# Stick-breaking attention of a hybrid decoder step: one head at a time, or both heads of a query block side by side

## The reference, cut to what matters

```
def _sb_block(q, k, v, bias, q_pos, k_pos):
    """Stick-breaking weights for one query block. q: [B,H,Q,d]; k, v: [B,H,K,d] (f32); bias: [H]."""
    z = jnp.einsum('bhqd,bhkd->bhqk', q, k) * (SB_HEAD_DIM ** -0.5) + bias[None, :, None, None]
    mask = k_pos[None, :] < q_pos[:, None]
    log_beta = jax.nn.log_sigmoid(z)
    log_rest = jnp.where(mask, jax.nn.log_sigmoid(-z), 0.0)
    tail = lax.cumsum(log_rest, axis=3, reverse=True) - log_rest
    A = jnp.where(mask, jnp.exp(log_beta + tail), 0.0)
    return jnp.einsum('bhqk,bhkd->bhqd', A, v)
...
    proj = h @ W['w_in'][l]
    qa, fa, ia, ga, qb, kb, vb, uc, gl = jnp.split(proj, _split_points(), axis=-1)
...
    ob = _sb_attention(qb, k_all, v_all, W['sb_bias'][l], q_pos, k_pos)
...
    u = ua * jax.nn.sigmoid(ug)
    c = _causal_dwconv(u_full, W['conv_w'][l], W['conv_b'][l])
```

## Time and profile before

| | |
|---|---|
| median of 3 runs | 2314.67 us (2312.46 to 2316.16) |
| span of the profiled execution | 2321.0 us |
| TensorE matmul / weight load busy | 93% / 86% |
| VectorE / ScalarE / GpSimd busy | 46% / 26% / 25% |
| chain that ended last | TensorE 85%, VectorE 7%, ScalarE 5% |
| the four groups, A and B stage together | 1098.6 us, 99.4 to 1198.0 |

### The profile page before, as it was taken

One profiled execution on the slowest core, in us unless ns is written; L12 is line 12 of the kernel. 1 busy time (PEld: TensorE's weight loads), 2 busy tenths in 40 slices (PEclk: granted clock), 3 DMA queues, 4 the chain that ended last, 5 costly groups with the idle time before them and its releaser, 6 DMA issues.

```text
span 2321.0 us, 31837 instructions
## 1 busy us (share of the span) xinstructions
PE 2147.9 (93%) x12704; PEld 2005.6 (86%) x12704; DVE 1079.1 (46%) x1169; ACT 604.1 (26%) x760; POOL 589.4 (25%) x392
## 2 busy tenths in 40 slices
PE   6999999999999999999978889789999999999994
PEld 5887898878988899878968889579999999999993
DVE  4277555775367663765534652452222223222235
ACT  3234412343223432345123421220100101001011
POOL 1221112211111211211112232343232333323322
PEclk9997999989998999989989999899999999999997
DMA  4220204102131121312144333201111120111132
GB/s 141 57 93 28 58 28 127 52 19 67 47 114 37 48 56 58 101 39 58 38 159 149 111 102 120 102 14 55 32 50 41 41 59 29 52 45 36 54 106 79
DMA packets 203987, 156.89 MB, mean 68 GB/s; under 512 B 15730, under 2 KB 188402, under 8 KB 203890
## 3 DMA queue, kind: packets, MB, share of 16 engines
q1 hardware_dynamic: 201698, 146.89, 20.4%
q10 hardware_dynamic: 2192, 8.65, 1.0%
HBM read 120.16 MB, written 35.35 MB: 67 GB/s over the span
## 4 chain that ended last, share of the span: by engine, by line
PE 85%; DVE 7%; ACT 5%; issue 1%; DMA 1%; POOL 0%; POOLq 0%; SPq 0%; DVEq 0%; ACTq 0%
PE psum L364 69%; PE psum L601 4%; PE psum L621 3%; PE psum L666 3%; PE psum L612 2%; PE psum L569 1%; DVE hid L1482 1%; PE psum L648 1%; DVE mix L1467 1%; PE psum L630 1%; DVE arena L1170 1%; DVE x_again L1461 0%; DMA conv_full<-c_d 0%; DVE hid_lo L1484 0%; DVE mix L1457 0%
## 5 line engine op out<-in xcount | busy, mean ns | idle before, releaser
L364 PE MATMUL psum<-h_hi,w_hi 128*128 128x352 f32 x2400 | 541.7, 334 | 37.1 <-DVE h_lo L1174 10.9
L364 PE MATMUL psum<-h_hi,w_lo 128*128 128x352 f32 x2400 | 525.7, 327 | 0.0
L364 PE MATMUL psum<-h_lo,w_hi 128*128 128x352 f32 x2400 | 525.6, 328 | 0.0
L364 PEld LDWEIGHTS psum<-h_hi,w_hi 128*128 128x128 f32 x2400 | 412.1, 193 | 75.9 <-issue 53.1
L364 PEld LDWEIGHTS psum<-h_hi,w_lo 128*128 128x128 f32 x2400 | 419.8, 191 | 0.0
L364 PEld LDWEIGHTS psum<-h_lo,w_hi 128*128 128x128 f32 x2400 | 416.3, 192 | 0.0
L341 POOL CAST w_hi<-w_raw 128x1024 fp32r<-128x1024 f32 x60 | 71.9, 1198 | 913.7 <-PE psum L364 895.1
L354 POOL CAST w_hi<-w_raw 128x512 fp32r<-128x512 f32 (+1 forms) x128 | 96.5, 754 | 732.5 <-PE psum L364 643.3
L356 POOL TENSOR_TENSOR w_lo<-w_raw,w_hi 128x512 fp32r<-128x512 f32 (+1 forms) x128 | 229.7, 1794 | 10.3
L1140 ACT ACTIVATE hid<-psum 128x1056 f32<-128x1056 f32 x32 | 33.7, 1054 | 583.1 <-PE psum L364 583.1
L364 PE MATMUL psum<-hid_hi,w_hi 128*128 128x352 f32 x768 | 166.4, 325 | 10.8 <-DVE hid_lo L1484 10.8
(11 more groups left out here) (226 smaller groups left out, 2459.8 us busy)
## 6 DMA issues: line engine op xcount, KB each, us to landing
w_raw<-in_w_in SPq DMA_DIRECT2D x60, 512.0 KB, 4.0
w_raw<-in_w_ff SPq DMA_DIRECT2D x32, 512.0 KB, 4.0
w_raw<-in_w_ff SPq DMA_DIRECT2D x64, 256.0 KB, 2.7
g_d<-gate_logits SPq DMA_DIRECT2D x24, 528.0 KB, 2.7
gates<-g_d SPq DMA_DIRECT2D x24, 528.0 KB, 3.6
arena<-in_xT SPq DMA_DIRECT2D x8, 528.0 KB, 7.0
x_again<-in_xT SPq DMA_DIRECT2D x1, 4224.0 KB, 13.8
x_d<-x_again ACTq DMA_DIRECT2D x8, 528.0 KB, 2.7
```

The source lines that it names most:

```text
L364: mm = pe.matmul(ps[:, b0 + g, 0:GW], w[:, slot, k, :], x[:, k, g * GW:(g + 1) * GW], start=(k == 0 and w is wh and x is xh), stop=(k == k ...
```

## The change

Scores and values of a query block q are done for both heads at once. `scores(p, q, c)` computes a chunk of up to 512 keys for head 0 into bank 3 and for head 1 into bank 4, in pieces of 256 that alternate between the two (partitions 0 to 63 and 64 to 127 of q and k). Blocks 4 to 7 have two chunks; since both heads take one bank each, chunk 1 can only be computed once ScalarE has read chunk 0. `values(p, q)` alternates the heads' 64-column tiles for each key block. The buffers for that are a fourth `zb` (the tile `ug`) and a second staged transpose (the tile `ua`), both free once the convolution input is formed.

The A stage now loops over q = 0 to 8. The units are given out by contraction tile: `fill(n)` does the next n tiles. In each q TensorE does: scores of chunk 0, transposes of block q-1 head 0, 2 tiles, scores of chunk 1 (q >= 4), sample work, 2 tiles, transposes of block q-1 head 1, 3 tiles, values of block q-1, 1 tile. That is one unit per q, nine in the A stage instead of eight. In the B stage 40 tiles are left for the 12 places (4, 4, then eight times 3, then 4, 4).

On ScalarE, each q begins with the copy of unit q-1 and ends with the exp of block q, head 1. VectorE in each q masks, taps and clips head 0, then head 1, taps, tail sum of head 0, taps, tail sum of head 1: four taps as in two steps before.

The diff, cut to its core:

```
+QB = TP // P
+Z_CHUNKS = [q if q < 4 else 4 + 2 * (q - 4) for q in range(QB + 1)]
+A_FILL = (2, 2, 3, 1)
+H_FILL = (4, 4, 3, 3, 3, 3, 3, 3, 3, 3, 4, 4)
...
-            def scores(p, i):
...
+            def scores(p, q, c):
+                chunk = Z_CHUNKS[q] + c
+                if chunk:
+                    z_read.wait(pe, p, 2 * chunk)
+                n = min(512, P * (q + 1) - 512 * c)
+                for a in range(0, n, 256):
+                    w = min(256, n - a)
+                    for e in range(2):
+                        rows = slice(DH * e, DH * e + DH)
+                        mm = pe.matmul(ps[:, 3 + e, a:a + w], qT[rows, q * P:(q + 1) * P],
+                                       kT[rows, 512 * c + a:512 * c + a + w], start=True, stop=True)
                 mm.then_inc(z_ready.sem, 1)
...
+            def values(p, q):
+                at_ready.wait(pe, p, 2 * q + 2)
+                if q:
+                    o_read.wait(pe, p, q)
+                for kb in range(q + 1):
+                    for e in range(2):
+                        mm = pe.matmul(ps[DH * e:DH * e + DH, 7, (q % 4) * P:(q % 4 + 1) * P],
+                                       vtok[:, kb, DH * e:DH * e + DH], atv[e][:, kb * P:(kb + 1) * P],
+                                       start=(kb == 0), stop=(kb == q))
                 mm.then_inc(av_done.sem, 1)
...
+                at_k = [0]
+                def fill(n):
+                    for _ in range(n):
+                        jj, k = divmod(at_k[0], KD)
+                        if jj < units(more):
+                            unit_part(PRE + jj, p, (k,))
+                            at_k[0] += 1
...
+                for q in range(QB + 1):
+                    if q < QB:
+                        scores(p, q, 0)
+                    if q == 1:
                         v_staged.wait(pe, p, 1)
+                    if q:
+                        turn_a(p, 2 * q - 2)
+                    fill(A_FILL[0])
+                    if 4 <= q < QB:
+                        scores(p, q, 1)
+                    if q == 1:
                         sample_scores(p)
+                    if q == 3:
                         sample_turn(p)
+                    if q == 4:
                         sample_values(p)
+                    fill(A_FILL[1])
+                    if q:
+                        turn_a(p, 2 * q - 1)
+                    fill(A_FILL[2])
+                    if q:
+                        values(p, q - 1)
+                    fill(A_FILL[3])
...
+                for q in range(QB + 1):
+                    if q:
+                        stage_unit(q - 1, p, more)
+                    if q < QB:
+                        if q == 1:
+                            u_ready.wait(act, p, 1)
+                        read_scores(q, 0)
+                    if q:
+                        stage_at(q - 1, 0)
+                    if 4 <= q < QB:
+                        read_scores(q, 1)
+                    if q < QB:
+                        softplus(q, 0)
...
+                    if q:
+                        stage_at(q - 1, 1)
+                    if q < QB:
+                        softplus(q, 1)
+                        weights_of(q, 0)
...
+                    if q:
+                        av_done.wait(act, p, q)
...
+                    if q < QB:
+                        weights_of(q, 1)
+                if more:
+                    kv_stored.wait(act, p, 32)
+                stage_unit(8, p, more)
...
-                    if j in (0, 2, 4):
-                        stage_unit(A_UNITS + j // 2, p, more)
+                    if j in (0, 3):
+                        stage_unit(9 + j // 3, p, more)
...
+                def scores_read(q, e):
+                    i, n = 2 * q + e, P * (q + 1)
+                    z, l = zb[2 * (q % 2) + e][:, 0:n], lb[e][:, 0:n]
+                    z_read.wait(dve, p, 2 * Z_CHUNKS[q + 1] - 1 + e)
...
+                for q in range(QB):
+                    scores_read(q, 0)
+                    scores_read(q, 1)
...
                     tap()
+                    tail_sum(q, 0)
+                    tap()
+                    tail_sum(q, 1)
```

More of the change, by code:

```diff
@@ L589, in _ @@
             ats = A(A_ATS, 192).rearrange("p (g n) -> p g n", g=3)
-            def scores(p, i):
-                qb, e = divmod(i, 2)
-                rows = slice(DH * e, DH * e + DH)
-                if i:
-                    z_read.wait(pe, p, i)
-                if i == 8:
-                    zs_read.wait(pe, p, 1)
-                nk = P * (qb + 1)
-                for a in range(0, nk, 512):
-                    n = min(512, nk - a)
-                    mm = pe.matmul(ps[:, 3 + a // 512, 0:n], qT[rows, qb * P:(qb + 1) * P], kT[rows, a:a + n],
-                                   start=True, stop=True)
+            def scores(p, q, c):
[9 more added lines that the diff above has]
+                                       kT[rows, 512 * c + a:512 * c + a + w], start=True, stop=True)
                 mm.then_inc(z_ready.sem, 1)
@@ L611, in turn_a @@
                 for kb in range(i // 2 + 1):
-                    mm = pe.transpose(banks(5, 1024)[:, kb * P:(kb + 1) * P], zb[i % 3][:, kb * P:(kb + 1) * P], ident)
+                    mm = pe.transpose(banks(5, 1024)[:, kb * P:(kb + 1) * P],
+                                      zb[2 * (i // 2 % 2) + i % 2][:, kb * P:(kb + 1) * P], ident)
                 mm.then_inc(t_done.sem, 1)
-            def values(p, i):
-                qb, e = divmod(i, 2)
-                at_ready.wait(pe, p, i + 1)
-                if e == 0 and qb:
-                    o_read.wait(pe, p, qb)
-                for kb in range(qb + 1):
-                    mm = pe.matmul(ps[DH * e:DH * e + DH, 7, (qb % 4) * P:(qb % 4 + 1) * P],
-                                   vtok[:, kb, DH * e:DH * e + DH], atv[:, kb * P:(kb + 1) * P],
-                                   start=(kb == 0), stop=(kb == qb))
+            def values(p, q):
[7 more added lines that the diff above has]
+                                       start=(kb == 0), stop=(kb == q))
                 mm.then_inc(av_done.sem, 1)
@@ L911, in stage_unit @@
                     stage(PRE + jj, p, *B_DST[jj - A_UNITS])
-            zb = [A(o, 1024) for o in A_Z]
+            zb = [A(o, 1024) for o in A_Z] + [ug[:, 0:1024]]
             lb = [A(o, 1024) for o in A_L]
@@ new lines, in read_scores, with softplus @@
+                def read_scores(q, c):
+                    z_ready.wait(act, p, Z_CHUNKS[q] + c + 1)
+                    n = min(512, P * (q + 1) - 512 * c)
+                    for e in range(2):
+                        act.activation(zb[2 * (q % 2) + e][:, 512 * c:512 * c + n], bank(3 + e, n), IDN,
+                                       bias=sbp[:, e:e + 1]).then_inc(z_read.sem, 1)
+                def softplus(q, e):
+                    i, l = 2 * q + e, lb[e][:, 0:P * (q + 1)]
+                    e_ready.wait(act, p, i + 1)
+                    act.activation(l, l, ACT.Exp).then_inc(exp1.sem, 1)
+                    exp1.wait(act, p, i + 1)
+                    act.activation(l, l, ACT.Ln, bias=1.0).then_inc(ln_ready.sem, 1)
@@ L1007, in group @@
                 qk_ready.wait(act, p, 1)
-                if more:
-                    kv_stored.wait(act, p, 32)
-                    u_ready.wait(act, p, 1)
                 for j in range(NL):
@@ L1025, in group @@
                     .then_inc(kdt_staged.sem, 1)
-                stage_unit(A_UNITS + 4, p, more)
+                stage_unit(12, p, more)
                 if more:
@@ L1039, in group @@
                 act.activation(A(B_RS, T), A(B_RS, T), ACT.Exp, scale=-0.5).then_inc(rs_ready.sem, 1)
-                stage_unit(A_UNITS + 5, p, more)
+                stage_unit(13, p, more)
                 if more:
@@ L1269, in group @@
                 t_done.wait(dve, p, 16)
-                av_done.wait(dve, p, 16)
+                av_done.wait(dve, p, QB)
                 os_done.wait(dve, p, 1)
```

164 lines of the change are left out of this document (58 added, 106 removed).

## The result

The changed kernel takes **2381.4 us** (median of 4 runs, 2380.9 to 2382.7) against 2315.4 us of the kernel before beside it: a ratio of **1.0284, 95% interval 1.0269 to 1.0299**, 66 us slower. The profiled execution spans 2380.9 us against 2321.0.

A forecast was written before the change was run, and what follows sets the result against it. A chain through VectorE's block and ScalarE's exp and copy was to bind late A-stage turns. A 183.2 plus B 100.4 made 283.6 us a group, 9 over 274.65; four groups add 36 to 2314.7, giving 2351 us, range 2303 to 2386.

The forecast's parts named there:

- The mechanism: A stage, q = 5 to 8: TensorE waits at the unit's first tile for ScalarE's copy, 15 to 20 us a group.
- F(5): Moment TensorE starts unit 5's first tile, after its wait for ScalarE's copy of unit 4; forecast 22.0 us after unit 4's.
- the ring: A-stage chain per turn: unit tiles, scores, read, VectorE's block, exp, copy, next unit; 23.1 to 23.2 us for q = 7.
- case D: The forecast itself: TensorE waits for the unit copy in q = 5 to 8; 2325 to 2378 us, chance 0.60.
- rival C: Score and value half tiles run one after the other, not together: 8 us a group more, 2384 us, chance 0.12.
- The walk up to F(4): Group 1's A stage summed turn by turn until TensorE starts unit 4's first tile: 71.8 us.
- cache wait: A stage, second turn: the sample's scores wait for the last cache page load, 3.4 us.
- the split: GpSimd's splitting of the next weights slows VectorE's tail sums beside it; taken as 0.8 us a turn.
- The clock: TensorE's clock halves after a stop of 6 us; 1.7 us each for q = 6, q = 7 and the tail.
- What stands behind F(8): A stage after unit 8's first tile starts: tiles, transposes and values 14.8 us, plus clock 1.7.
- Rival A: TensorE binds, not the chain: A stage 160 us, group 260.7, whole 2259 us; chance 0.06.
- Rival B: Chain binds, but clock stays up and splits cost nothing: no change, 2306 to 2325 us; chance 0.18.

The follow-up runs named there:

- kernel 1: Changed kernel with ScalarE's exp of the second head moved into the next turn, behind the unit copy and the score reads: 2288.3 us, ratio 0.9881.
- kernel 11: Fastest kernel (2218.8 us, late exp plus TensorE reordering) with the second head's exp back ahead of the unit copy: 2353.5 us, ratio 1.0157.
- kernel 3: Changed kernel with GpSimd splitting only the first of a unit's eight contraction tiles inside the groups (outputs not valid): 2333.0 us, ratio 1.0074.
- kernel 6: Changed kernel with TensorE kept busy in its three long waits by repeated score products: 2366.6 us, ratio 1.0208.
- kernel 4: Changed kernel with heads not alternated, all of head 0's score or value tiles and then head 1's: 2394.7 us, ratio 1.0337.
- kernel 5: kernel 1 with the heads' score and value tiles not alternated: 2290.9 us, ratio 0.9873.
- kernel 10: Late-exp kernel with TensorE's fills and sample steps reordered (2238.6 us), now with the heads' score and value tiles not alternated: 2248.5 us, ratio 0.9701.

## Why the prediction was right, and where it was off

**The mechanism** was forecast and is shown. The waits stand where it put them (the unit's first tile, for ScalarE's copy), three of 7 to 8 us a group, 22.8 us in sum, where "4 to 7 us, three or four times a group, 15 to 20 us in sum" was written, with VectorE busy through them. There is none at F(5), which the prediction counted in. Opening the ring by one moved instruction (kernel 1) takes them all away; closing it again under a better order elsewhere (kernel 11) brings them all back.

**The range** held by more than the mechanism. The measured 2381 us lies above the 2325 to 2378 that the prediction gave to its own case D, and nearest to the 2384 of rival C, whose mechanism the rows below refute. The stated range reached to 2386 only because C was in it: that the time fell inside is luck to that extent.

**The size.** 36 us were forecast and 66 measured. Of the 66, some 5 come from the base: the profiled execution of the kernel before was 5.6 us over its median, and the changed kernel's was not. The stages grew by 61. Term by term, for group 1, through which the prediction walked:

- The half tiles overlap fully: the timeline of the changed kernel's TensorE has a pair of value tiles every 0.11 us, each pair starting together.

```profile
549.32 0.27 PE L626 MATMUL psum<-arena 128*64 128x128 f32 x1
549.33 0.27 PE L626 MATMUL psum<-ua,arena 128*64 128x128 f32 x1
549.43 0.27 PE L626 MATMUL psum<-arena 128*64 128x128 f32 x1
549.44 0.27 PE L626 MATMUL psum<-ua,arena 128*64 128x128 f32 x1
```

  In the kernel before, one such tile alone took 0.11 us. A group's values keep TensorE busy for 9.6 us where they took 20.0, its scores for 11.0 where they took 21.8. Rival C falls.
- The walk up to F(4) was right to a microsecond: F(1) 16.2 (forecast 16.1), F(2) 36.8 (37.5, where the terms written add to 37.2), F(3) 52.9 (52.9), F(4) 72.4 (71.8), with the cache wait 2.9 us (3.4) and the sample's 3.0 (3.3). The other groups reach F(4) at 73.6 to 74.0. There the split met VectorE's second tail sum, on the ring ahead of F(1): in group 2 its scan of 128 keys took 2.52 us, in group 1 0.42. So the near hit at F(1) is group 1's luck.
- The turns from F(4) to F(8) hold **the term that was mis-sized**: 22.7, 23.8, 27.5 and 27.6 us against 22.0, 22.0, 25.3 and 25.6, 6.7 us in group 1 and 6.0 in the mean of four. Most of it is the split beside VectorE. I took 0.8 us a turn from one instruction that had met only the end of a split: it ran from 214.29 to 215.90, and the cast ahead of that subtraction ended at 215.09. The rows from F(6) to F(7) above show 0.79 on the tap that met the cast (1.03 where such a tap takes 0.24 alone) and 2.02 on the scan that started within the subtraction, 2.81 together; kernel 3 gives 2.1 to 2.7 for each turn from F(5) on, and nothing for the one before. The prediction named the case ("one that starts within it can wait its whole length") and priced the milder one. GpSimd starts when a unit ends and VectorE's scan follows at a fixed distance, so the two meet in the same way in all four groups; that is no average of chances.
- The clock: 1.7 us were taken for q = 6, for q = 7 and for the tail. The low stretches at the waits were 6.8, 10.2 and 10.2 us long, not 3.4, but lie in part within the waits, and kernel 6 gives up to 2 us per turn. Between F(4) and F(5) the clock was low for 6.8 us too; in kernel 6 it was 3.4, and that turn took 21.1 us in place of 22.7. The clock is the smaller part of the miss.
- What stands behind F(8) took 16.6 us (16.5), so the A stage was 190.6 us instead of 183.2.
- B stages: 98.8 against 100.4. The wait before product 0 became 4.0 us (4.6; 3.1 before), the two unit ends 1.2 each as written. The mean of four is 99.1: 5 us less than forecast in all.

Sum of the misses over the four groups, by their means: 4 x 7.7 in A less 4 x 1.3 in B, 26 us, and 36 + 26 = 62 against the 61 of the stages.

**The rivals.** Rival A, that TensorE would bind, needed "the chain 6 us shorter". Kernel 1 did that, and gave 2288, not 2259, because other waits then came to light; with these covered, and those of the B stage too, it is 2219. Rival B's free split and free clock are kernels 3 and 6: 49 and 15 us. If the two add, which no run tried and which is doubtful, since kernel 3 has less low clock too, that would have been no change, as B said. Neither is free.

The rule on the lock: the Trainium skill (SBUF — State Buffer, Who interferes with whom) says that a VectorE instruction with two inputs in SBUF and a GpSimd instruction that reads SBUF exclude each other, and that the one that starts first holds the port to its end. The trace agrees to about 0.1 us: the subtraction ended at 526.55 + 3.16 = 529.71, and the scan, whose two inputs lie in SBUF and which takes 2.02 alone, ended at 527.55 + 4.04 = 531.59, 1.9 later.

## To carry to other kernels

When work of two streams is put into one turn, write down for each in-order engine what stands behind each wait: here one exp that waits for VectorE stood ahead of a copy and of reads that were ready, and it cost 93 us as changed and 135 once the other waits were covered. Look for the turn's ring (who starts the turn, and what closes it) before counting busy time; a busy share of two thirds on VectorE (63% of the changed A stage) was enough to bind. And when a wait is removed, read the trace again: the next ones, each of 1 to 5 us and covered by cheap reordering of the filling work, were worth another 70 us.

## What the hardware showed that I had not expected

- Tiles of the two halves of the array overlap even when the program does not alternate them: with two score matmuls of one head ahead of two of the other, eight records took 1.14 us, as alternated (1.13). With eight value matmuls of one head first, those of the second began some 0.3 us before the first's last records. The Trainium skill (TensorE: Matmul & The Clock Gate, Part 3) says that matmuls start strictly in program order; the starts in the rows of kernel 4 do not agree: a record of the second head at 582.47 lies before three of the first head, at 582.57, 582.68 and 582.79 (float32, column halves). A float32 matmul leaves two records, so at least the first head's last matmul began after the second head's first. Here the measurement decides.
- Work added to TensorE's waits made the kernel 15 us faster (kernel 6). Work added where TensorE sets the turn did not show once (kernel 5, 0.9873 against 0.9881), and there the waits for the last exps were 2.2 us shorter in group 1 and the low clock 28 us shorter over the program; in kernel 10 such work cost some 10 us.
- A GpSimd split nearly doubles a VectorE scan that starts within it: 768 keys 3.78 us in place of 1.90, 896 keys 4.04 in place of 2.16 (changed kernel and kernel 3, the same in all four groups).
